# Seven-product (Strassen) gate and up projections in a hybrid decoder block, with all final rows after the last product

## The chip, the cores and the metric

The kernel runs on one core of one Trainium2 chip. The metric is the device time of one execution in microseconds (us), from runs repeated on the same chip; the kernel before takes 1517.94 us (median of 3 runs, 1517.23 to 1519.09). In the profile the engines are PE (TensorE, matmuls), PEld (its weight loads), DVE (VectorE), ACT (ScalarE), POOL (GpSimd) and SP (SyncE, which issues the DMAs).

## The reference

A decoder block on 1024 tokens of width 1024, all in float32. The change touches only its second part, the SwiGLU feed-forward layer with 2816 features, and the layer norm behind it:

```python
# token mixing (projection, convolution, windowed attention, gates, w_out), then
x = layer_norm(ALPHA * x + mix, ln1_g, ln1_b)
hid = silu(x @ w_gate) * (x @ w_up)        # (1024, 2816)
ffn = hid @ w_down                         # (1024, 1024)
x = layer_norm(ALPHA * x + ffn, ln2_g, ln2_b)
```

## The kernel before

Every product of two float32 matrices is made of three matmuls in a reduced-mantissa format: each operand is split into a high part (ACT copies it to that format) and a low part (the difference, made by POOL for weights and by DVE for activations), and high x high, high x low and low x high are added up in PSUM (`product`, lines 971 to 979). Activations lie channels by tokens, as `act_hi` and `act_lo`: 8 tiles of 128 channels, 1024 tokens in two halves of 512.

The feed-forward part works in 11 groups of two feature blocks of 128. For one group the gate and the up weights of both blocks are four tiles of 128 features (`gate_up`, L1132; `s` = 0 to 3, even for gate). A unit is one of these against one half of the tokens: 8 channel tiles x 3 = 24 matmuls of 128x512, so a group has 8 units or 192 matmuls. Behind each pair of units ACT takes the tanh (`silu`, L621), DVE makes gate times up (`hidden`, L896), ACT its high part and DVE its low part. `down` (L1141) then multiplies the two hidden blocks into the output: 16 units (8 output tiles x 2 halves) of 2 x 3 = 6 matmuls, 96 in all, and after each one DVE adds the bank to the residual `res` (`add_down`, L920). Each weight tile is loaded by SP (`load_ffn`), copied by ACT (`ffn_high_part`, L572) and subtracted by POOL (`ffn_low_part`, L400), one group ahead. All engines run their own instruction streams in order and wait for each other through semaphores.

The order on TensorE is: output projection of the mixing part (L1128), first-half units of group 0, into which the statistics of the first layer norm are woven (`mean`, `variance`, `spread`, L1094 to L1115), second-half units of group 0, `down` of group 0, first-half units of group 1, and so on. Before that norm's second half DVE runs `scale_residual(0)` (L866, L894), eight operations that bring the first half of the residual to its scaled and biased form; `scale_residual(1)` (L917) stands between `hidden(0, 0, 1)` and `hidden(0, 1, 0)`, and unit 15's addition to the residual (L881) behind `scale_residual(0)`.

The last group is different. Its output is made as finished rows (tokens on partitions), `last_rows` (L1173): per row block of 128 tokens and half of the channels four transposes of the residual and six matmuls of the last two hidden blocks. `row_stats`, `row_centre` and `row_scale` (DVE, ACT, DVE) and one POOL addition turn them into the output, which SP stores. The list `LAST` (L83) weaves rows 0, 1 and 2 between the four last second-half units; rows 3 to 7 come after them.

Of the kernel before, what the change touches and what calls it, by code (L numbers as in the profile page):

```python
# [21 lines left out]
F32R = mybir.dt.float32r  # L22
# [4 lines left out]
P = 128  # L27
# [32 lines left out]
def head_schedule():  # L60
# [4 lines left out]
    for u in range(2 * NT):  # L65
# [17 lines left out]
LAST = [("unit", 0), ("rows", 0), ("unit", 1), ("silu", 0), ("rows", 1), ("unit", 2), ("rows", 2), ("unit", 3),  # L83
        ("silu", 1)] + [("rows", i) for i in range(3, NB)]
# [13 lines left out]
def build(nc, x, w_in, conv_w, sinks, w_out, ln1_g, ln1_b, w_gate, w_up, w_down, ln2_g, ln2_b, out):  # L98
    ctx = ExitStack()
    with ctx:  # L100
# [27 lines left out]
        sb(ctx, "line_up", [P, 120])  # L128
# [41 lines left out]
        ln2_rows = sb(late, "ln2_rows", [P, 2, D])  # L170
        sb(late, "spare", [P, HALF])
        raw_b = sb(late, "raw_b", [P, 2, DT, P])
# [6 lines left out]
        with ExitStack() as st:  # L179
# [4 lines left out]
            raw_d = sb(st, "raw_d", [P, 2, D])  # L184
            hid_hi = sb(st, "hid_hi", [P, 2, S], F32R)
            hid_lo = sb(st, "hid_lo", [P, 2, S], F32R)
            tanh_g = sb(st, "tanh_g", [P, 2, HALF])
            hid = sb(st, "hid", [P, 2, HALF])
# [27 lines left out]
        n_hi_s, n_lo_s, scaled_s = sem("norm_hi_done"), sem("norm_lo_done"), sem("residual_scaled")  # L216
        fw_in = [sem(f"ffn_w_landed{i}") for i in range(6)]
# [38 lines left out]
        def ffn_raw(s):  # L256
            return raw_b[:, s] if s < 2 else raw[:, s - 2] if s < 4 else raw_d[:, s - 4]
# [6 lines left out]


# [19 lines left out]
        ROW_BANKS = [4, 6, 4, 6, 0, 2, 4, 6]  # L285

        def row_out(i):

            return raw_b[:, i % 4].rearrange("p t c -> p (t c)") if i % 4 < 2 else raw_d[:, i % 4 - 2]

        def row_banks(i):
            return ps[:, ROW_BANKS[i]:ROW_BANKS[i] + 2, :]


        @block.sync
        def _(sp):
# [21 lines left out]
            def load_ffn(g, s):  # L318
                if s < 4:
                    w = (w_gate, w_up)[s % 2]  # L320
                    src = w[0, :, bass.ds(g * (2 * P) + P * (s // 2), P)].rearrange("(t p) c -> p t c", p=P)
                else:
                    src = w_down[0, bass.ds(g * (2 * P) + P * (s - 4), P), :]
                sp.dma_start(ffn_raw(s), src).then_inc(fw_in[s], 16)

            for v in range(OUT_TILES):
                sp.wait_ge(w_lo_s, IN_TILES + v - 1)
                load_w(v % 2, w_out, P * (v % DT))
                if v == DT:
                    sp.wait_ge(merge_s, 2 * NKV)  # L330
                    load_ffn(0, 0)
                    load_ffn(0, 1)
            for s in (2, 3):
                sp.wait_ge(w_lo_s, IN_TILES + OUT_TILES - 3 + s)
                load_ffn(0, s)
            sp.wait_ge(out_s, OUT_TILES)
            load_ffn(0, 4)
# [881 lines left out]
```

## Time and profile before

| | |
|---|---|
| time, median of 3 | 1517.94 us |
| the profiled execution's own time | 1517.19 us |
| its span, first to last instruction | 1515.3 us |
| TensorE busy | 1491.6 us, 98% of the span, 6898 matmuls |
| VectorE, ScalarE, GpSimd busy | 46%, 28%, 26% |
| granted TensorE clock, mean | 0.994 |
| DMA, mean | 53 GB/s |

A matmul's length in the trace (0.39 us) holds its way through the array; the next one starts before it ends. What a matmul costs in a dense stream is the distance from start to start. A length with "x2" behind it is that of two merged instructions. The number in brackets at a row's end is the time for which the engine sat idle before, and who released it.

### The profile page before, as it was taken

Reading aid. Unit: us, or ns where it says so; the run is one execution under the profiler, and the core shown is the slowest. Engines: PE = TensorE matmul, PEld = TensorE weight load, DVE = VectorE, ACT = ScalarE, POOL = GpSimd, SP = SyncE. Lnnn points to the kernel's source line nnn. Section 1 sums busy time; section 2 is a strip of 40 time slices with the busy share of each in tenths; the row PEclk is TensorE's granted clock in tenths of the full one; section 3 lists DMA queues with packets and bytes.
Section 4 is the critical chain, followed back from the end, with each engine's and each line's share of the span. In section 5 each row is a group of like instructions: output and inputs, shape, how many; then the busy total and the mean of one; then the engine's idle time right before and its main releaser. Section 6 shows DMA issues by size and latency. Waiting matters only on the chain.

```text
span 1515.3 us, 18733 instructions
## 1 busy us (share of the span) xinstructions
PE 1491.6 (98%) x6898; PEld 1241.3 (82%) x6898; DVE 696.5 (46%) x1063; ACT 429.7 (28%) x803; POOL 396.5 (26%) x187
## 2 busy tenths in 40 slices
PE   9999999999999999989989999999999999999997
PEld 7888888888888888868868888888888888888885
DVE  3227662766366636679677231323323132332335
ACT  3424332433243324342444111211112121111223
POOL 2121132113211321136743121303213031221303
PEclk9999999999999999999999999999999999999999
DMA  5111111111111111113331110202111020211002
GB/s 168 56 50 34 42 42 47 36 42 42 45 38 42 42 44 39 42 42 111 97 98 55 57 55 28 83 0 83 49 34 55 28 83 12 71 55 55 0 14 98
DMA packets 127754, 80.07 MB, mean 53 GB/s; under 512 B 7792, under 2 KB 122480, under 8 KB 127728
## 3 DMA queue, kind: packets, MB, share of 16 engines
q1 hardware_dynamic: 127728, 79.73, 17.5%
q8 instruction: 16, 0.26, 0.1%
q14 instruction: 10, 0.08, 0.0%
HBM read 75.53 MB, written 4.19 MB: 53 GB/s over the span
## 4 chain that ended last, share of the span: by engine, by line
PE 96%; DVE 3%; ACT 1%; issue 0%; POOL 0%; ACTq 0%; DVEq 0%; POOLq 0%
PE ps L976 29%; PE ps L978 29%; PE ps L977 29%; PE ps L1085 2%; PE ps L1076 2%; PE ps L1068 1%; PE ps L1067 1%; DVE act_lo L850 1%; DVE m_lo L819 0%; DVE res L869 0%; DVE bn L939 0%; PE ps L991 0%; DVE res L860 0%; DVE raw_d L953 0%; PE ps L999 0%
## 5 line engine op out<-in xcount | busy, mean ns | idle before, releaser
L976 PE MATMUL ps<-act_hi,w_hi 128*128 128x512 f32 x1184 | 463.1, 391 | 1.1 <-DVE act_lo L674 1.1
L978 PE MATMUL ps<-act_hi,w_lo 128*128 128x512 f32 x1184 | 461.1, 389 | 0.0
L977 PE MATMUL ps<-act_lo,w_hi 128*128 128x512 f32 x1184 | 461.0, 389 | 0.0
L382 POOL TENSOR_TENSOR w_lo<-raw,w_hi 128x1024 fp32r<-128x1024 f32 x54 | 131.9, 2443 | 506.7 <-ACT w_hi L469 506.7
L978 PEld LDWEIGHTS ps<-act_hi,w_lo 128*128 128x128 f32 x1184 | 222.3, 188 | 46.7
L976 PEld LDWEIGHTS ps<-act_hi,w_hi 128*128 128x128 f32 x1184 | 222.4, 188 | 45.9 <-issue 1.3
L977 PEld LDWEIGHTS ps<-act_lo,w_hi 128*128 128x128 f32 x1184 | 222.5, 188 | 44.5
L923 DVE TENSOR_TENSOR res<-res,ps 128x512 f32<-128x512 f32 x160 | 109.5, 687 | 94.2 <-PE ps L978 94.2
L402 POOL TENSOR_TENSOR w_lo_b<-raw_b,w_hi_b 128x1024 fp32r<-128x1024 f32 x22 | 52.5, 2407 | 372.9 <-ACT w_hi_b L575 372.9
L976 PE MATMUL ps<-act_hi,w_hi_b 128*128 128x512 f32 x352 | 138.2, 393 | 0.0
L977 PE MATMUL ps<-act_lo,w_hi_b 128*128 128x512 f32 x352 | 137.3, 390 | 0.0
L978 PE MATMUL ps<-act_hi,w_lo_b 128*128 128x512 f32 x352 | 137.2, 390 | 0.0
L976 PE MATMUL ps<-hid_hi,wd_hi 128*128 128x512 f32 x320 | 124.5, 389 | 0.0
L977 PE MATMUL ps<-hid_lo,wd_hi 128*128 128x512 f32 x320 | 124.5, 389 | 0.0
L978 PE MATMUL ps<-hid_hi,wd_lo 128*128 128x512 f32 x320 | 124.5, 389 | 0.0
L901 DVE SCALAR_TENSOR_TENSOR hid<-tanh_g,ps 128x512 f32<-128x512 f32 x44 | 30.3, 688 | 169.3 <-ACT tanh_g L625 169.0
L905 DVE TENSOR_TENSOR hid<-hid,ps 128x512 f32<-128x512 f32 x44 | 30.3, 688 | 160.6 <-PE ps L978 160.3
L627 ACT ACTIVATE hid_hi<-hid 128x512 fp32r<-128x512 f32 x44 | 27.8, 632 | 232.0 <-DVE hid L905 232.0
L402 POOL TENSOR_TENSOR wd_lo<-raw_d,wd_hi 128x1024 fp32r<-128x1024 f32 x22 | 52.4, 2405 | 131.9 <-ACT wd_hi L575 131.9
L977 PEld LDWEIGHTS ps<-act_lo,w_hi_b 128*128 128x128 f32 x352 | 66.4, 189 | 14.3 <-issue 0.5
L976 PEld LDWEIGHTS ps<-act_hi,w_hi_b 128*128 128x128 f32 x352 | 66.4, 189 | 14.3 <-issue 0.5
L978 PEld LDWEIGHTS ps<-act_hi,w_lo_b 128*128 128x128 f32 x352 | 66.3, 188 | 13.8
(144 smaller groups left out, 1915.4 us busy)
## 6 DMA issues: line engine op xcount, KB each, us to landing
raw<-in_w_in SPq DMA_DIRECT2D x52, 512.0 KB, 3.8
raw_d<-in_w_down SPq DMA_DIRECT2D x22, 512.0 KB, 3.3
raw<-in_w_out SPq DMA_DIRECT2D x16, 512.0 KB, 3.6
raw_b<-in_w_gate SPq DMA_DIRECT2D x11, 512.0 KB, 3.8
raw_b<-in_w_up SPq DMA_DIRECT2D x11, 512.0 KB, 3.9
raw<-in_w_gate SPq DMA_DIRECT2D x11, 512.0 KB, 3.9
raw<-in_w_up SPq DMA_DIRECT2D x11, 512.0 KB, 4.0
xs<-in_x SPq DMA_DIRECT2D x8, 512.0 KB, 8.2
```

What stands on the lines that cost most here:

```text
L382: pool.tensor_tensor(w_lo[:, slot], raw[:, slot], fp(w_hi[:, slot]), ALU.subtract).then_inc(w_lo_s, 1)
L402: pool.tensor_tensor(ffn_lo(s), ffn_raw(s), fp(ffn_hi(s)), ALU.subtract).then_inc(fw_lo_s, 1)
L627: act.activation(hid_hi[:, t, half(h)], hid[:, t], ACT.Copy, scale=0.5).then_inc(silu_s, 1)
L850: dve.scalar_tensor_tensor(out=act_lo[:, m, half(q)], in0=res[:, m, half(q)], scalar=lnb[:, m:m + 1], in1=fp(act_hi[:, m, half(q)]), op0=A ...
L901: dve.scalar_tensor_tensor(out=hid[:, t], in0=tanh_g[:, t], scalar=1.0, in1=ps[:, 2 * t, :], op0=ALU.add, op1=ALU.mult).then_inc(hid_s, 1)
L905: dve.tensor_tensor(hid[:, t], hid[:, t], ps[:, 2 * t + 1, :], ALU.mult).then_inc(hid_s, 1)
L923: dve.tensor_tensor(res[:, m, half(h)], res[:, m, half(h)], ps[:, 4 + v % 4, :], ALU.add).then_inc(add_s, 1)
L976: pe.matmul(bank, w_h(t), a_hi(t), start=(t == 0), stop=False)
L977: pe.matmul(bank, w_h(t), a_lo(t), start=False, stop=False)
L978: last = pe.matmul(bank, w_l(t), a_hi(t), start=False, stop=(t == tiles - 1))
L1076: last = pe.transpose(ps[:, TURN + kb, blk(g)], prob[:, g, blk(kb)], ident[:])
L1085: last = pe.matmul(ps[:, OUT, :], vs[:, n - 1 + kb, :], part[:, kb], start=(kb == kbs[0] and part is pt_hi), stop=(kb == 1 and part is pt_lo))
```

## The change

Of the 11 groups, group 0 stays as it was. The 20 feature blocks of groups 1 to 10 ("pairs": the gate and the up tile of one block) are computed by one level of the seven-product scheme (Strassen's, in Winograd's form). The 2 x 2 blocks of the left matrix are gate and up weights by first and second half of the channels (A11, A12, A21, A22, each 512 channels by 128 features), those of the right one the two halves of the channels by the two halves of the tokens. Seven products of 4 channel tiles x 3 = 12 matmuls stand for eight, so 84 matmuls in place of 96 for a feature block. Around them:

- Sums of right blocks are made once, after group 0's norm: on DVE `token_sums` (five operations on 128x512 for each of 4 tiles) and `depth_difference` (4, from the third on each waits for the POOL subtraction two before), on ACT 16 copies to the high format, on POOL 8 subtractions. One right block replaces `act_hi`/`act_lo` of the first four channel tiles, second token half.
- Sums of left blocks are made for every feature block on POOL (4 operations on 128x512); ACT makes 7 high parts of 128x512 and POOL 7 low parts, into a ring of four, in place of two of 128x1024 each.
- The products land in four PSUM banks (BX, BY, BZ, BW); ACT copies the first one out, DVE combines them with 7 operations, then `tanh`, gate times up and the split go on as before (5 more on DVE, 4 on ACT). TensorE waits in front of products 0, 1, 3, 4 and 6 for a bank to be read.
- The down projection stays the same, after every second feature block. Its weights now come through one buffer `raw_d` in place of two.
- `scale_residual` is gone; the scale is folded into the first `add_down`, the bias into the last.
- All eight `last_rows` follow the last product.

```diff
-LAST = [("unit", 0), ("rows", 0), ("unit", 1), ("silu", 0), ("rows", 1), ("unit", 2), ("rows", 2), ("unit", 3),
-        ("silu", 1)] + [("rows", i) for i in range(3, NB)]
+PAIRS = 2 * (NG - 1)
+FIRST_HIGH, SECOND_SUM, SECOND_LOW, THIRD_DIFF, FIRST_LOW, FIRST_SUM, FOURTH_DIFF = range(7)
+U2, U3, UP0, GATE0, HID0, LOW0, UP1, PART1, SUM1, GATE1, HID1, LOW1 = range(1, 13)
...
@@ SP @@
-            sp.wait_ge(out_s, OUT_TILES)
-            load_ffn(0, 4)
-            load_ffn(0, 5)
+            sp.wait_ge(stat_s, 5)
+            load_down(0)
+            sp.wait_ge(wd_lo_s, 1)
+            load_down(1)
+            sp.wait_ge(last_lo_s, 4)
+            for c in (A11, A21, A22, A12):
+                load_block(c, 2)
...
@@ POOL, per feature block @@
+                pool.tensor_tensor(w_sum[:, 0], wide(block_raw(A21)), wide(block_raw(A22)), ALU.add).then_inc(sum_s, 1)
+                pool.tensor_tensor(w_sum[:, 1], w_sum[:, 0], wide(block_raw(A11)), ALU.subtract).then_inc(sum_s, 1)
+                low(FIRST_HIGH)
+                low(SECOND_SUM)
+                low(SECOND_LOW)
+                pool.tensor_tensor(wide(block_raw(A21)), wide(block_raw(A11)), wide(block_raw(A21)),
+                                   ALU.subtract).then_inc(sum_s, 1)
+                low(THIRD_DIFF)
+                low(FIRST_LOW)
+                pool.tensor_tensor(w_sum[:, 1], wide(block_raw(A12)), w_sum[:, 1], ALU.subtract).then_inc(sum_s, 1)
+                low(FIRST_SUM)
+                low(FOURTH_DIFF)
...
@@ POOL, once, before the pairs @@
+            down_low_part(0, 0, 0)
+            for t in range(4):
+                pool.wait_ge(dhi_s, t + 1)
+                pool.tensor_tensor(a3_lo[:, t], w_sum[:, t % 2], fp(a3_hi[:, t]), ALU.subtract).then_inc(dlo_s, 1)
+            down_low_part(0, 0, 1)
...
@@ ACT, once @@
+            for t in range(4):
+                act.wait_ge(asum_s, 3 * t + 1)
+                act.activation(a1_hi[:, t], u3[:], ACT.Copy).then_inc(ahi_s, 1)
+                act.wait_ge(asum_s, 3 * t + 2)
+                act.activation(a2_hi[:, t], w_sum[:, 0], ACT.Copy).then_inc(ahi_s, 1)
+            act.wait_ge(out_s, OUT_TILES)
+            down_high_part(0, 0, 0)
+            silu(1, 0)
+            for t in range(4):
+                act.wait_ge(diff_s, t + 1)
+                act.activation(a3_hi[:, t], w_sum[:, t % 2], ACT.Copy).then_inc(dhi_s, 1)
+            down_high_part(0, 0, 1)
+            act.wait_ge(f_s, 8)
...
...
@@ ACT, per feature block, even ones (odd ones: the next block's parts come last) @@
+                first_copy(i, c)
+                product_high(i, c, 4)
+                down_high_part(i, 2 * (c // 2) + 2, c % 2)
+                product_high(i, c, 5)
+                product_high(i, c, 6)
+                    product_high(i, c + 1, 0)
+                    gate_tanh(i, c, 0)
+                    product_high(i, c + 1, 1)
+                    hidden_high(i, c, 0)
+                    product_high(i, c + 1, 2)
+                    product_high(i, c + 1, 3)
+                    gate_tanh(i, c, 1)
+                    hidden_high(i, c, 1)
...
@@ DVE, once @@
             hidden(0, 1)
+            for t in range(4):
+                token_sums(t)
+            hidden(1, 0)
+            for t in range(4):
+                depth_difference(t)
+            hidden(1, 1)
...
@@ PE @@
+            def down(i, c, h, m):
                 if m == 0:
+                    pe.wait_ge(wd_lo_s, i * 4 + (2 * c + 2))
...
+            def pair_product(i, c, j):
+                if j == FIRST_HIGH:
+                    pe.wait_ge(pair_s, before + GATE0)
+                elif j == SECOND_SUM:
+                    pe.wait_ge(pair_s, before + SUM1)
+                elif j == THIRD_DIFF:
+                    pe.wait_ge(pair_s, now + U2)
+                elif j == FIRST_LOW:
+                    pe.wait_ge(s1_s, i * 4 + (c + 1))
+                elif j == FOURTH_DIFF:
+                    pe.wait_ge(pair_s, now + U3)
...
-            for step, n in LAST:
-                if step == "unit":
-                    second_half(NG - 1, n)
-                elif step == "rows":
-                    last_rows(n)
+            for n in range(NB):
+                last_rows(n)
```


## Rows read from the trace of the kernel before

**Rows 1.** The page: busy shares, granted clock in 40 slices, shares of the last chain.
```profile
PE 1491.6 (98%) x6898; PEld 1241.3 (82%) x6898; DVE 696.5 (46%) x1063; ACT 429.7 (28%) x803; POOL 396.5 (26%) x187
...
PEclk9999999999999999999999999999999999999999
...
PE 96%; DVE 3%; ACT 1%; issue 0%; POOL 0%; ACTq 0%; DVEq 0%; POOLq 0%
```

**Rows 2.** The timeline at a unit's end: start, length, engine, line, operation, idle before.
```profile
1007.58 0.39 PE L978 MATMUL ps<-act_hi,w_lo_b 128*128 128x512 f32 x1
...
1007.81 0.39 PE L976 MATMUL ps<-act_hi,w_hi 128*128 128x512 f32 x1
...
1008.10 0.69 DVE L905 TENSOR_TENSOR hid<-hid,ps 128x512 f32<-128x512 f32 x1 [4.03 <-PE ps L978]
...
1008.82 0.63 ACT L627 ACTIVATE hid_hi<-hid 128x512 fp32r<-128x512 f32 x1 [5.57 <-DVE hid L905]
```

**Rows 3.** All instructions of line 923 on VectorE: lengths in ns, first and last start.
```profile
L923 DVE TENSOR_TENSOR res<-res,ps x160: 679/687/689, 825.1 to 1432.3; 128x512 f32<-128x512 f32 x160
```

**Rows 4.** Groups by line, 1000 to 1400 us: count, busy us, mean ns, idle before.
```profile
L402 POOL TENSOR_TENSOR wd_lo<-raw_d,wd_hi 128x1024 fp32r<-128x1024 f32 x12 | 28.5, 2397 | 65.6 <-ACT wd_hi L575 65.6
...
L625 ACT ACTIVATE tanh_g<-ps 128x512 f32<-128x512 f32 x25 | 15.0, 598 | 97.5 <-PE ps L978 97.5
...
L575 ACT ACTIVATE w_hi<-raw 128x1024 fp32r<-128x1024 f32 x12 | 11.9, 1043 | 0.0
```

**Rows 5.** The timeline of GpSimd, 742 to 780 us.
```profile
754.37 1.28 POOL L415 TENSOR_TENSOR acc<-acc,res 128x512 f32<-128x512 f32 x1
755.62 2.85 POOL L426 TENSOR_TENSOR wd_lo<-raw,wd_hi 128x1024 fp32r<-128x1024 f32 x1
...
770.92 1.46 POOL L415 TENSOR_TENSOR acc<-acc,res 128x512 f32<-128x512 f32 x1
775.71 1.26 POOL L415 TENSOR_TENSOR acc<-acc,res 128x512 f32<-128x512 f32 x1 [3.33 <-DVE res L881]
```

**Rows 6.** The timeline of VectorE, 740 to 860 us.
```profile
754.39 1.81 DVE L850 SCALAR_TENSOR_TENSOR act_lo<-res,lnb,act_hi 128x512 fp32r<-128x512 f32 x1
756.13 0.73 DVE L860 SCALAR_TENSOR_TENSOR res<-res,lng,ps 128x512 f32<-128x512 f32 x1
756.79 2.23 DVE L850 SCALAR_TENSOR_TENSOR act_lo<-res,lnb,act_hi 128x512 fp32r<-128x512 f32 x1
...
768.83 6.20 DVE L869 TENSOR_SCALAR res<-res,lnb 128x512 f32<-128x512 f32 x8
774.96 0.67 DVE L881 SCALAR_TENSOR_TENSOR res<-res,ps 128x512 f32<-128x512 f32 x1
...
808.88 0.69 DVE L907 SCALAR_TENSOR_TENSOR hid_lo<-hid,hid_hi 128x512 fp32r<-128x512 f32 x1 [0.70 <-ACT hid_hi L627]
```

**Rows 7.** The timeline of TensorE, 760 to 800 us.
```profile
777.12 2.05 PE L1097 MATMUL ps<-acc,mean_of 128*128 128x512 f32 x2 [5.18 <-POOL acc L415]
...
779.39 0.63 PE L977 MATMUL ps<-act_lo,w_hi_b 128*128 128x512 f32 x1
```

**Rows 8.** The timeline of TensorE, 799 to 803 us.
```profile
801.09 0.39 PE L976 MATMUL ps<-act_hi,w_hi_b 128*128 128x512 f32 x1
```

**Rows 9.** The timeline of TensorE, 1486.2 to 1491 us.
```profile
1486.63 0.60 PE L1187 MATMUL ps<-ident,res 128*128 128x128 f32 x4
...
1488.46 0.60 PE L1187 MATMUL ps<-ident,res 128*128 128x128 f32 x4
```

**Rows 10.** The timeline of VectorE, 1440 to 1515 us.
```profile
1498.65 1.29 DVE L939 BATCH_NORM_STATS2 bn<-ps 128x6 f32<-128x512 f32 x2
...
1507.00 1.29 DVE L939 BATCH_NORM_STATS2 bn<-ps 128x6 f32<-128x512 f32 x2
```

**Rows 11.** DMA issues: queue, count, KB each, median us from issue to landing.
```profile
raw_d<-in_w_down SPq DMA_DIRECT2D x22, 512.0 KB, 3.3
...
ln_rows<-in_ln_b SPq DMA_DIRECT2D x1, 512.0 KB, 6.0
```

More of the change, by code:

```diff
@@ L168, in build @@
             sq = sb(st, "sq", [P, 2, HALF])
[L170 to L172 removed]
+        u3 = sb(late, "u3", [P, HALF])
+        w_sum = sb(late, "w_sum", [P, 2, HALF])
+        raw_d = sb(late, "raw_d", [P, D])
+        with ExitStack() as st:
+            raw_b = sb(st, "raw_b", [P, 2, DT, P])
+        t_g = sb(late, "t_g", [P, 2, HALF])
+        u_st = sb(late, "u_st", [P, 2, HALF])
         with ExitStack() as st:
@@ new lines, in _ @@
+            down_high_part(0, 0, 0)
[6 more added lines that the diff above has]
+            for t in range(4):
+                act.wait_ge(asum_s, 3 * t + 3)
+                act.activation(act_hi[:, t, half(1)], fourth[:, t * HALF:(t + 1) * HALF], ACT.Copy).then_inc(last_hi_s, 1)
@@ L648, in row_centre @@
+            act.wait_ge(f_s, 8)
+            for j in range(4):
+                product_high(0, 0, j)
+            with act.Fori(0, (NG - 2) // 2) as i:
+                for c in range(4):
+                    pair_act(i, c)
+            for c in range(4):
+                pair_act((NG - 2) // 2, c, c < 3)
             def row_centre(i):
@@ L935, in row_stats @@
+            with dve.Fori(0, (NG - 2) // 2) as i:
+                for d in range(2):
+                    pair(i, 2 * d)
+                    pair(i, 2 * d + 1, lambda v: add_down(i, d + 1, v, "plain"))
+            last = (NG - 2) // 2
+            pair(last, 0)
+            pair(last, 1, lambda v: add_down(last, 1, v, "biased"))
+            pair(last, 2)
+            pair(last, 3)
             def row_stats(i):
@@ new lines, in _ @@
+            for s in range(4):
+                pe.wait_ge(hid_s, 3 * (s // 2) + 1 + s % 2)
+                gate_up(1, s, (lambda t: pe.wait_ge(n_lo_s, DT + t + 1)) if s == 0 else None)
+            for h in range(2):
+                for m in range(DT):
+                    down(0, 0, h, m)
+            def pair_product(i, c, j):
+                n = 7 * c + j
+                before = i * 48 + STEPS_OF * c
+                now = i * 48 + STEPS_OF * (c + 1)
+                pe.wait_ge(pl_s, i * 28 + (n + 1))
+                if j == FIRST_HIGH:
[8 more added lines that the diff above has]
+                    pe.wait_ge(pair_s, now + U3)
+                bank = {FIRST_HIGH: BX, SECOND_SUM: BY, SECOND_LOW: BW, THIRD_DIFF: BY, FIRST_LOW: BX, FIRST_SUM: BZ,
+                        FOURTH_DIFF: BY}[j]
+                out, on = ps[:, bank, :], j in (THIRD_DIFF, FIRST_LOW)
+                for t in range(4):
+                    hi, lo = ring(w_hi, n)[:, t], ring(w_lo, n)[:, t]
+                    b_hi, b_lo = right(j, t)
+                    pe.matmul(out, hi, b_hi, start=(t == 0 and not on), stop=False, skip_group_check=True)
+                    pe.matmul(out, hi, b_lo, start=False, stop=False, skip_group_check=True)
+                    last = pe.matmul(out, lo, b_hi, start=False, stop=(t == 3), skip_group_check=True)
+                last.then_inc(prod_s, 1)
```

460 lines of the change are left out of this document (325 added, 135 removed).

## The prediction

> **What bounds the kernel now.** I read the page first: TensorE is busy 98% of the span, its granted clock stands near full in all 40 slices, and the chain that ended last is TensorE for 96% [rows 1]. So the question is how many matmuls there are, what one costs, and where TensorE would have to wait. A busy share says nothing of the cost of one, so I went to the timeline: starts lie 0.23 us apart while each row is 0.39 long [rows 2]. The exact pitch comes from the downward additions: 160 of them, the first at 825.1, the last at 1432.3 [rows 3]. The last lies 15 units of 6 matmuls behind the first of its own group, and nine groups of 288 matmuls lie between the firsts: 9 x 288 + 90 = 2682 matmuls in 607.2 us is 0.2264, and allowing 0.7 us by which the very first addition ran late, 0.2267 us each (12 matmuls: 2.72). That is the pitch of a stream without a hole across nine groups and their loop ends; TensorE truly bounds this stretch.
>
> **Part 1: the matmuls that go.** 12 per feature block, 20 blocks: 240 x 0.2267 = 54.4 us, all on the path. The bounds are narrow, since product and down matmuls have the form of those removed: 54 to 55.
>
> **Part 2: `scale_residual(0)` goes.** Its eight operations take DVE 768.83 to 775.03, then comes unit 15's addition, 0.67 us, then POOL's last channel sum 775.71 to 776.97 [rows 5, 6], and TensorE's `mean` starts at 777.12 after 5.18 us idle [rows 7]. Without them the addition is through at about 769.6. Next late is POOL: its sixth sum starts at 770.92 behind a weight subtraction [rows 5]; two sums of 1.3 and 0.1 between them end at 773.6, and `mean` starts at 773.8: 3.3 us gained. After that idle time the granted clock is at its lower level, 1.2 GHz: a matmul ends 0.43 behind the one before instead of 0.23 [rows 7] for some five of them, and the two of `mean` take 2.05. With under 2 us idle some of this may go: 0 to 1.9 us, I take 1.0. Sum 4.3 (bounds 3.3 to 5.2).
>
> **Part 3: sums of the activations, before the pairs.** This is the dear part. The clock of before less 4.3 from here. Second-half units started at 801.09 [rows 8], now 796.8, and their 96 matmuls end at 818.6. DVE is through with `hidden(0, 1)` at 809.57 - 4.3 = 805.3 [rows 6]. `token_sums`: dependent DVE operations of 0.69 [rows 2] need about 0.8 each with the wait; per tile three of them, then two low parts that find ACT's copies (0.63, starting 0.03 behind their source [rows 2]) done, 3.7 us; four tiles: 14.8, to 820.1. ACT then still has `down_high_part` (1.04 [rows 4]), done at 819.5, and the tanh (0.60 [rows 4]); `hidden(1, 0)` takes until 823.0. Then come the differences: two at once, to 824.3; the third needs POOL's first `a3_lo` (ACT's copy at 824.3, POOL 1.26 [rows 5]) and finds POOL on the second, 826.8; the fourth at 828.2; ACT's last copy 828.8, POOL's last 830.6. Only behind that stands `down_low_part(0, 0, 1)`: ACT's copy at 829.9 (the one buffer was free at 822, and a load lands in 3.3 [rows 11]), POOL's 2.40 [rows 4], from 830.6 to 833.0. The first `down` waits for exactly this. TensorE stands still from 818.6 to 833.1: 14.5 us. Before, a group's `down` found its weights done long ago. I bound it by 10 (dependent operations at 0.66 and no contention) and 20 (a landing of 6.0 [rows 11] and every DVE operation held up by POOL once). The clock afterwards starts low again, as in Part 2: 1.5 us more (0 to 2). The rest of this preparation is hidden: POOL's last subtractions end near 838.6, the pair's four blocks are loaded and summed by 854, and `down` runs until 833.1 + 1.5 + 21.8 = 856.4. The down additions start late, near 836.5, as DVE first ends `hidden(1, 1)`; the fifth down unit, at 838.5, needs one of them: just there.
>
> **Part 4: do the pairs run without holes?** Time 0 is the start of an even block's product 0; product j ends at 2.72(j + 1), and others see it 0.29 later (1008.10 against 1007.81 [rows 2]). POOL's work per block is 11 operations of 1.25 [rows 5] and one of 2.40, 16.2 us against TensorE's 19.0: the fullest engine beside it. Worse, POOL and DVE exclude each other when DVE has two inputs in SBUF. DVE's L850 at 754.39 took 1.81 instead of 0.7: it ran when POOL's operation of 754.37 ended at 755.65; and that of 756.79 took 2.23, until POOL's 2.85 long one (2.40 elsewhere) let go. L860, whose second input is in PSUM, took 0.73 in the middle of it [rows 5, 6]. Five of the twelve DVE operations (HID0, LOW0, GATE1, HID1, LOW1) are of the first kind.
>
> The Trainium skill ("SBUF — State Buffer", Who interferes with whom) says the same as a rule: two SBUF inputs on DVE and a reading GpSimd operation take turns, for a whole instruction. Without such turns the chain below would have about 1.3 us more to spare and the sum would not change.
>
> The tight place is where an odd block follows an even one with no `down` between. POOL: the sixth low part after ACT's copy at 9.1, `down_low_part` until 12.7, first sum 13.95, second 15.35, then DVE's HID0 takes its turn to 16.0, low 0 until 17.2 (TensorE wants it at 19.05), DVE's LOW0 to 17.8, low 1 until 19.05 (wanted at 21.8), low 2 until 20.3, third sum 21.55. ACT: copy 3 22.2, only then the tanh 22.8. DVE: GATE1 after POOL's low 3, 24.1; HID1 24.9; ACT 25.6; LOW1 26.3; U2 of the odd block 27.0. TensorE's product 3 of that block wants U2 at 19.05 + 8.16 = 27.2. So it just fits, with 0.2 us; a further turn lost to POOL costs up to 1.25 once in each of the ten double blocks: 0 to 12 us, I take 1.0 in all. All other waits have over 1.4 us: first copy 26.2 for 29.9, low 4 28.1 for 29.9, LOW0 of the odd block 37.6 at worst for `down` at 38.1, LOW1 43.5 for its second half at 49; the additions follow from 43.5 and stay ahead of the four banks. While `down` runs (21.8 us) the next block's first four parts are made. What covers Part 1 is thus this slack; where it's gone, products wait one by one.
>
> **Part 5: the end.** Before: row 3 starts on TensorE at 1486.63, the span ends 28.7 later; the three woven rows cost 2 x 1.83 = 3.66 each on TensorE [rows 9]: 39.7 us. After the last product, now: SUM1, tanh, GATE1, HID1, copy, LOW1, 4.55 us; DVE's first `row_stats` starts there (TensorE's row 0 is done at 3.7). Rows then follow each other at the pace of the DVE and ACT chain, (1507.00 - 1498.65) / 2 = 4.18 [rows 10], seven times 29.3, and from the last one's start to the end of the span are 8.3: 42.2. Loss 2.5 us (1 to 5): three rows more at 4.18 instead of 3.66, and the start. The rows of the norm's parameters land in 6.0 [rows 11], within the last seven-product block.
>
> **Sum.** -54.4 - 4.3 + 14.5 + 1.5 + 1.0 + 2.5 = -39.2: span 1515.3 to 1476.1. The profiled execution took 1517.19, 1.9 more than its span, so 1478.0; the median of the runs is 0.75 above that execution: 1478.7, so 1479 us.
>
> **The rivals.**
> A, main: TensorE stays the bound in the pairs, one stall of some 14 us before them. 1479, from 1470 to 1488. Chance 0.66.
> B: the turns of POOL and DVE, or a product's low part, come late in each double block. For it speaks the 0.2 us of slack, and that TensorE's stall moves everything behind it; against it that U2 late by a turn only costs that turn. 1 to 3 us for each of ten, where A has 0.1: 1488 to 1508, likeliest 1494. Chance 0.17.
> C: no real stall at the preparation (DVE or the down weights sooner than worked out): 1479 less 10 to 15, 1464 to 1469. For it only that each step of Part 3 is an estimate; against, the order of the streams. Chance 0.09.
> D, slower: every DVE operation and POOL exclude each other, those with an input in PSUM too. Then the 38.1 us of a double block hold some 24.8 us of POOL work and 24 x 0.66 = 15.8 of DVE: 40.6, and the ring's slack is used up by handoffs, 5 us or more per double block; from 4 us each on the 39 are gone. 1529. Against it stands the 0.73 us of L860 [rows 6]. Chance 0.04.
> E: the change doesn't do what it says: TensorE's pitch in the products rises above 0.227, as with accumulation into a bank that is read between, by 0.01 x 1680 = 17 us: 1496. The same form of matmul in `down` switches banks every 6 without loss. Chance 0.04.
>
> The Trainium skill ("TensorE: Matmul & The Clock Gate", Why this matters for your kernels) warns that idle gaps between bursts of matmuls bring the slow clock; by that rule the stall of Part 3 is followed by a slow start, and the trace agrees at 777 us.
>
> **Range and chances.** A with its bounds, B's likelier half and the upper end of C make 1467 to 1500: this leaves out the end of C, the upper third of B, D. A measurement of this kernel can tell about 0.2% (3 us). Faster 0.95, same 0.01, slower 0.04.
>
> **What would show it.** Part 1: 6658 matmuls instead of 6898 at an unchanged pitch of 0.227. Part 2: `mean` starts about 3 us sooner after the last unit. Part 3: TensorE idle 14 us ahead of the first `down`, released by POOL's `wd_lo`. Part 4: a double block with its `down` takes 168 + 96 = 264 matmuls, 59.9 us, from one to the next; more means B, and the idle row names its releaser. Part 5: rows 4.2 us apart, the last product 42 us before the end. The prediction is wrong if a double block takes over 61 us, or if the first `down` starts within 5 us of the last unit.

## The result and the profile after

The changed kernel takes 1477.92 us (median of 4 runs, 1475.69 to 1479.79) against 1518.4 us (4 runs) beside it: a ratio of 0.9735, 95% interval 0.9723 to 0.9746. The forecast was 1479 us. The profiled execution is the slowest of the four, 1479.79 us with a span of 1478.0; a second profile of the same kernel, called after_again below, has a span of 1474.3.

The page of after (busy time and share of each engine, then the chain that ended last); TensorE has 240 matmuls fewer than in [rows 1] and still is busy for 97% of the span:

```profile
PE 1440.5 (97%) x6658; PEld 1198.4 (81%) x6658; DVE 798.7 (54%) x1194; ACT 486.7 (33%) x935; POOL 602.4 (41%) x375
...
PE 90%; DVE 4%; POOL 2%; ACT 2%; issue 1%; DMA 0%; SPq 0%; ACTq 0%; DVEq 0%; POOLq 0%
```

Some stretches of after: first the end of the norm, the stall and the first down projection, then two of the 60 us stretches of the pairs, the first and the last but one. Columns: length, busy time of TensorE, its weight loads, VectorE, ScalarE and GpSimd with the number of instructions in brackets, then granted clock, DMA share and GB/s:

```profile
775.00:800.00 25.00, 24.26 (x110) 19.80 (x109) 17.29 (x26) 12.74 (x19) 5.76 (x4) 0.93 0.07 22
...
821.00:835.00 14.00, 0.50 (x3) 0.21 (x2) 7.38 (x11) 7.51 (x13) 10.06 (x7) 0.60 0.11 37
835.00:860.00 25.00, 25.00 (x99) 20.41 (x100) 12.70 (x19) 3.05 (x5) 14.01 (x11) 0.88 0.32 95
860.00:920.00 60.00, 60.00 (x266) 49.70 (x265) 28.87 (x41) 15.95 (x26) 33.85 (x24) 1.00 0.18 53
...
1340.00:1400.00 60.00, 60.00 (x266) 49.70 (x265) 29.96 (x40) 15.86 (x26) 33.75 (x24) 1.00 0.18 53
```

From 860 to the end of the last product TensorE has no hole in any stretch. The ScalarE copy that each feature block has once gives the distance of the blocks (durations in ns, then the first and the last start):

```profile
L820 ACT ACTIVATE u_st<-ps x20: 579/592/598, 862.5 to 1423.3; 128x512 f32<-128x512 f32 x20
```

20 copies, the first at 862.5, the last at 1423.3. The 560.8 us between them serve below to compare kernels; they are no exact pitch, since the first copy starts 3.0 behind the start of its block on TensorE (859.49) and the last 6.2 (1417.09). The pitch is in TensorE's own rows: 2544 matmuls from the start of the first product at 859.49 to the end of the last at 1436.13, 0.2267 each: to four digits the pitch that the prediction takes from [rows 3]. The holes that there are, by TensorE's waits (releaser, us in total, times, longest):

```profile
PE ps L1289 <- POOL wd_lo L543: 13.5, 1, 13.5
PE ps L1289 <- DVE m_lo L1042: 5.4, 3, 2.0
PE ps L1410 <- POOL acc L504: 1.8, 1, 1.8
...
PE ps L1418 <- DVE sq_acc L1056: 0.7, 1, 0.7
```

The 13.5 us are the stall ahead of the first down projection; the 5.4 us behind `m_lo` are in both kernels. The stall's surroundings on TensorE (start, length, idle before), to be read beside [rows 7, 8]:

```profile
820.91 0.39 PE L1291 MATMUL ps<-act_hi,w_lo 128*128 128x512 f32 x1
834.79 0.79 PE L1289 MATMUL ps<-hid_hi,wd_hi 128*128 128x512 f32 x1 [13.50 <-POOL wd_lo L543]
835.39 0.63 PE L1290 MATMUL ps<-hid_lo,wd_hi 128*128 128x512 f32 x1
...
840.87 0.39 PE L1291 MATMUL ps<-hid_hi,wd_lo 128*128 128x512 f32 x1
```

and the chain that released it, on GpSimd, where the last weight subtraction stands behind four of the activations' (to be read with [rows 5] for its lengths):

```profile
821.46 2.51 POOL L543 TENSOR_TENSOR wd_lo<-raw_d,wd_hi 128x1024 fp32r<-128x1024 f32 x1 [37.45 <-ACT wd_hi L781]
826.17 2.49 POOL L583 TENSOR_TENSOR a_lo<-w_sum,a_hi 128x512 fp32r<-128x512 f32 x2 [2.20 <-ACT a_hi L793]
829.94 2.49 POOL L583 TENSOR_TENSOR a_lo<-w_sum,a_hi 128x512 fp32r<-128x512 f32 x2 [1.29 <-ACT a_hi L793]
832.40 2.34 POOL L543 TENSOR_TENSOR wd_lo<-raw_d,wd_hi 128x1024 fp32r<-128x1024 f32 x1
```

The end, VectorE's `row_stats` of the first rows, answers to [rows 10]:

```profile
1440.44 1.29 DVE L1255 BATCH_NORM_STATS2 bn<-ps 128x6 f32<-128x512 f32 x2
...
1444.63 1.29 DVE L1255 BATCH_NORM_STATS2 bn<-ps 128x6 f32<-128x512 f32 x2
```

The pace is 4.19 us a row, and the last product ends at 1436.13, 41.9 us before the end of the span.

### The profile page after: what moved, and what is told of

Its sections match the earlier page's. It is cut to its first block, busy times and chain, and to the rows that moved or that the text cites. A ratio compares the mean times of both kernels' runs of the same rounds, so it can differ in the third digit from the quotient of the medians.

```text
span 1478.0 us, 19122 instructions
## 1 busy us (share of the span) xinstructions
PE 1440.5 (97%) x6658; PEld 1198.4 (81%) x6658; DVE 798.7 (54%) x1194; ACT 486.7 (33%) x935; POOL 602.4 (41%) x375
## 3 DMA queue, kind: packets, MB, share of 16 engines
HBM read 75.53 MB, written 4.19 MB: 54 GB/s over the span
## 4 chain that ended last, share of the span: by engine, by line
PE 90%; DVE 4%; POOL 2%; ACT 2%; issue 1%; DMA 0%; SPq 0%; ACTq 0%; DVEq 0%; POOLq 0%
PE ps L1289 19%; PE ps L1290 19%; PE ps L1291 19%; PE ps L1505 9%; PE ps L1504 9%; PE ps L1506 9%; PE ps L1398 2%; PE ps L1389 2%; PE ps L1381 1%; PE ps L1380 1%; DVE rows L1269 1%; POOL acc L504 1%; DVE bn L1255 1%; ACT rows L882 1%; DVE m_lo L1042 1%
## 5 line engine op out<-in xcount | busy, mean ns | idle before, releaser
L559 POOL TENSOR_TENSOR w_lo<-raw,w_hi 128x512 fp32r<-128x512 f32 x80 | 108.5, 1357 | 234.8 <-ACT w_hi L814 234.8
L1291 PEld LDWEIGHTS ps<-act_hi,w_lo 128*128 128x128 f32 x864 | 162.5, 188 | 34.4
L1289 PEld LDWEIGHTS ps<-act_hi,w_hi 128*128 128x128 f32 x864 | 162.8, 188 | 33.6 <-issue 1.3
L1290 PEld LDWEIGHTS ps<-act_lo,w_hi 128*128 128x128 f32 x864 | 162.7, 188 | 32.1
L1289 PE MATMUL ps<-hid_hi,wd_hi 128*128 128x512 f32 x320 | 125.9, 393 | 13.5 <-POOL wd_lo L543 13.5
L1504 PE MATMUL ps<-a_hi,w_hi 128*128 128x512 f32 x240 | 93.4, 389 | 0.0
L1505 PE MATMUL ps<-a_lo,w_hi 128*128 128x512 f32 x240 | 93.4, 389 | 0.0
L1506 PE MATMUL ps<-a_hi,w_lo 128*128 128x512 f32 x240 | 93.4, 389 | 0.0
L559 POOL TENSOR_TENSOR w_lo<-w_sum,w_hi 128x512 fp32r<-128x512 f32 x60 | 81.8, 1371 | 11.3 <-ACT w_hi L814 11.3
L1289 PEld LDWEIGHTS ps<-hid_hi,wd_hi 128*128 128x128 f32 x320 | 60.7, 190 | 26.6 <-POOL wd_lo L543 13.9
L612 ACT ACTIVATE w_hi<-raw 128x1024 fp32r<-128x1024 f32 x54 | 57.0, 1056 | 70.4 <-PE ps L1291 69.8
```

The lines of the kernel that those rows point to most:

```text
L559: pool.tensor_tensor(wide(ring(w_lo, n)), src, fp(wide(ring(w_hi, n))), ALU.subtract).then_inc(pl_s, 1)
L612: act.activation(w_hi[:, slot], raw[:, slot], ACT.Copy).then_inc(w_hi_s, 1)
L1289: pe.matmul(bank, w_h(t), a_hi(t), start=(t == 0), stop=False)
L1290: pe.matmul(bank, w_h(t), a_lo(t), start=False, stop=False)
L1291: last = pe.matmul(bank, w_l(t), a_hi(t), start=False, stop=(t == tiles - 1))
L1504: pe.matmul(out, hi, b_hi, start=(t == 0 and not on), stop=False, skip_group_check=True)
```

## The experiments

All ratios are against the kernel before, with 95% intervals; "against the changed kernel" compares medians (1476.91 us for after_again in the first group of runs). Differences of 1 us are at the edge of what the runs tell.

**The base.** after_again is the changed kernel unaltered, no diff.

> The changed kernel once more, as the base of the three beside it on the same chip. Theory: 1478 us within 3, with some 13.5 us of idle TensorE ahead of the first down product.

Measured: 1476.91 us (5 runs, 1476.09 to 1478.65), ratio 0.9733 (0.9720 to 0.9746), TensorE idle 13.5 us behind `wd_lo` as before. Its span is 3.7 us shorter than that of the first profile: `token_sums` begins at 805.4 instead of 807.8, and the first product at 855.8 instead of 859.5. The clock makes all of that. Behind the last of the three waits for `m_lo`, ahead of everything that the change touches, the first profile has twelve matmuls at a distance of 0.43 us, this one eight and the profile of before seven; behind the wait of 0.7 us for `variance` the first profile has six and this one none; behind the stall it is thirteen and about seven. The three places make 0.7, 1.7 and 1.3 us. The first of them in the first profile:

```profile
678.39 0.80 PE L1289 MATMUL ps<-m_hi,w_hi 128*128 128x512 f32 x1 [1.80 <-DVE m_lo L1042]
...
683.68 0.45 PE L1289 MATMUL ps<-m_hi,w_hi 128*128 128x512 f32 x1
```

**1. The weights first.** Is the stall only that of the two down weight tiles?

```diff
@@ ScalarE @@
+            act.wait_ge(out_s, OUT_TILES)
+            down_high_part(0, 0, 0)
             for t in range(4):
+                if t == 3:
+                    down_high_part(0, 0, 1)
                 act.wait_ge(asum_s, 3 * t + 1)
...
-            act.wait_ge(out_s, OUT_TILES)
-            down_high_part(0, 0, 0)
             silu(1, 0)
...
-            down_high_part(0, 0, 1)
@@ GpSimd @@
             down_low_part(0, 0, 0)
+            down_low_part(0, 0, 1)
...
-            down_low_part(0, 0, 1)
```

> Changed kernel, in which the two down weight tiles of group 0 are copied (ScalarE) and subtracted (GpSimd) before and between the sums of the activations, not after them. Nothing else moves. Theory: TensorE starts down at about 821, right behind the last unit, does four of its units and then waits for VectorE's first addition, which still comes after hidden(1, 1) near 837: the stall changes its name and shrinks from 13.5 to about 11 us, and 5 to 6 us are gained in all, since four units of down (5.4 us) lie before it. Rival: the weights are all that is late; then the whole stall and its slow clock go, 16.5 us.

Measured: 1477.38 us (4 runs), ratio 0.9733 (0.9718 to 0.9748): nothing gained against the changed kernel, where I had expected 5 to 6 us. The stall did change its name; TensorE, the four early down units and the wait for VectorE's first addition:

```profile
820.29 0.50 PE L1290 MATMUL ps<-hid_hi,wd_hi 128*128 128x512 f32 x1 [1.26 <-POOL wd_lo L543]
...
838.91 0.80 PE L1290 MATMUL ps<-hid_hi,wd_hi 128*128 128x512 f32 x1 [12.88 <-DVE res L1181]
```

But the idle time did not shrink (1.3 + 12.9 us). The weights' subtraction on GpSimd now lies beside `token_sums`. VectorE and GpSimd, same kernel:

```profile
806.24 2.77 DVE L1133 SCALAR_TENSOR_TENSOR w_sum<-res,lnb,u 128x512 f32<-128x512 f32 x1
...
818.05 2.74 DVE L1131 TENSOR_TENSOR u<-res 128x512 f32<-128x512 f32 x1
```

```profile
805.90 2.56 POOL L543 TENSOR_TENSOR wd_lo<-raw_d,wd_hi 128x1024 fp32r<-128x1024 f32 x1 [22.53 <-ACT wd_hi L781]
817.72 2.52 POOL L543 TENSOR_TENSOR wd_lo<-raw_d,wd_hi 128x1024 fp32r<-128x1024 f32 x1 [9.25 <-ACT wd_hi L781]
```

An operation with two inputs in SBUF that takes 0.75 elsewhere took 2.77, ending 0.5 behind GpSimd's 2.56 long one, and another that takes 0.69 took 2.74. That puts 4 us into the chain that ends in the first addition; later waits take up some of it, and the addition comes 32.7 us behind the start of `token_sums` (838.18 - 805.52) instead of 30.0.

The expected 5 to 6 us were also never there. Counted from the start of `token_sums`, the changed kernel's down projection starts at 27.0 us (834.79 - 807.77). With the weights early its fifth unit waits for the end of the first addition, at 30.7: four units of work (5.4 us) are done by then, but the rest starts 3.7 us later, so that only 1.7 us were to be gained. The turns took 2.7, and the first product comes 51.4 us behind the start of `token_sums` (856.9 - 805.5) in place of 50.4 in after_again. Neither theory holds in its size: the weights are not all that is late, and with VectorE's order as it is, moving them alone has little to give.

**2. Weights first and VectorE's work in another order.** The edit of experiment 1, and on VectorE the following; ScalarE and GpSimd follow, with `silu(1, 1)` and its copies ahead of those of `a3`:

```diff
             hidden(1, 0)
-            for t in range(4):
-                depth_difference(t)
-            hidden(1, 1)
...
-            for v in range(2 * DT):
-                add_down(0, 0, v, "first")
+            for v in range(4):
+                add_down(0, 0, v, "first")
+            hidden(1, 1)
+            for v in range(4, 2 * DT):
+                add_down(0, 0, v, "first")
+                if v < DT:
+                    depth_difference(v - 4)
```

> As weights_early, and VectorE takes four down additions before hidden(1, 1) and puts the four depth differences between the next additions; ScalarE and GpSimd follow that order. Theory: no stall of over 1 us is left ahead of the pairs, 13.7 us of idle time and 2.9 us of slow clock are gained: 16.6 us less than the changed kernel, 1461. Rival: the work is only pushed to the start of the pairs, where products wait for it: gain under 10 us.

Measured: 1468.78 us (4 runs), ratio 0.9672 (0.9657 to 0.9687), 8.1 us less than the changed kernel; half of what was expected. From the start of `token_sums` to the first product it takes 40.3 us (808.4 to 848.7), against 50.4 in after_again and 51.7 in the first profile; without any hole it would be 35.1. TensorE's waits name what is left:

```profile
PE ps L1294 <- DVE res L1176: 2.0, 2, 1.0
...
PE ps L1294 <- POOL wd_lo L543: 1.3, 1, 1.3
...
PE ps L1509 <- DVE inv L1194: 0.8, 1, 0.8
```

Four short waits in place of a long one, 4.1 us, at a granted clock of 1.00, and in this kernel too two VectorE operations of 2.77 and 2.74 us took turns with GpSimd. So the stall is that of a packed VectorE: between the start of `token_sums` and the first product it is busy for 35.6 of the 40.3 us here (32.6 of 51.7 in the first profile), where TensorE's own work takes 35.1, and each turn with GpSimd lengthens it. As the profiles differ in the clock before this place, the 10 to 11 us of the stretch and the 8.1 us of the medians are not the same number. It was not pushed into the pairs (560.4 us between first and last copy, as before).

**3. What the stall's slow clock costs.** 56 matmuls into a bank that is free fill most of the idle stretch:

```diff
+            for n in range(56):
+                pe.matmul(ps[:, 4, :], act_hi[:, 0, 0:P], act_hi[:, 0, half(0)], start=True, stop=True)
             for h in range(2):
                 for m in range(DT):
                     down(0, 0, h, m)
```

> Changed kernel with 56 extra matmuls of 128x512 into a bank that nobody reads, between group 0's last unit and its first down product: 12.7 us of work inside the stall of 13.7. Theory: TensorE keeps the granted clock of 2.4 GHz, the first down products run at 0.227 from the start and 2.9 us are gained although 56 matmuls are added. Rival: the slow start of down has another cause (the first reading of new weights): no gain, or a loss where the extra matmuls outlast the stall.

Measured: 1475.37 us (5 runs, 1475.25 to 1475.59), ratio 0.9720 (0.9707 to 0.9733). 1.5 us less than after_again, with 56 matmuls more. The windows (columns as above) of after_again and then of this kernel:

```profile
832.00:842.00 10.00, 9.58 (x36) 7.82 (x37) 6.02 (x9) 1.27 (x2) 5.80 (x5) 0.82 0.28 78
```

```profile
818.00:832.00 14.00, 14.00 (x64) 11.51 (x62) 7.88 (x11) 8.30 (x14) 8.75 (x6) 1.00 0.11 37
832.00:842.00 10.00, 9.01 (x40) 7.23 (x39) 6.48 (x10) 1.33 (x3) 6.70 (x5) 1.00 0.20 58
```

TensorE now waits 1.0 us for `wd_lo`, the granted clock stays at 1.00 over the whole stretch and the slow start is gone, so its cause is the idle time. I had expected 2.9 us, the figure of the first profile; 1.5 us is what the medians give, and all five runs lie below all five of after_again. This is also the kernel whose runs lie closest together (0.3 us, where the changed kernel's spread over 4). How much of that is chance in five runs is not shown: the slow matmuls behind `m_lo` and `variance` come before the filled stretch, so the filling can't have changed them.

**4. How near GpSimd is to being the bound in the pairs.** One more operation in odd, then in even feature blocks (`c % 2 == 0` in the second kernel):

```diff
+                if c % 2 == 1:
+                    pool.tensor_tensor(w_sum[:, 0], wide(block_raw(A21)), wide(block_raw(A22)), ALU.add).then_inc(twice_s, 1)
+                    pool.wait_ge(twice_s, i * 2 + (c // 2 + 1))
                 pool.tensor_tensor(w_sum[:, 0], wide(block_raw(A21)), wide(block_raw(A22)), ALU.add).then_inc(sum_s, 1)
```

> Changed kernel in which GpSimd does the first weight sum of every odd feature block twice, one operation of 128x512 (1.25 us, 1.4 with the wait) more in the tight place of the prediction. Theory: U2 of the odd block was ready 0.5 us before TensorE wanted it, so product 3 now starts some 0.9 us late in each of ten double blocks: 9 us more than the changed kernel, 1487. Rival: GpSimd works ahead by a ring of four and one operation is hidden: within 1 us of the changed kernel.

> The same extra operation in every even block instead, whose first sums fall into the down products (21.8 us). Theory: hidden, within 1 us of the changed kernel. Rival: GpSimd's total load is what counts: as much slower as with the odd blocks.

Measured: odd 1486.14 us (4 runs), ratio 0.9793 (0.9778 to 0.9808); even 1477.93 us (4 runs), ratio 0.9736 (0.9721 to 0.9751). 9.2 us more than the changed kernel for the odd blocks, 1.0 for the even ones, and first to last copy takes 570.3 us instead of 560.8: 0.95 us per double block. The size and the rule (the second of two neighbouring blocks is tight, the one behind a down projection is free) are as worked out. The place is another. (SUM1, HID0, LOW0 and U2 are steps of VectorE's work on a feature block, by the names in the diff of the change.) VectorE and TensorE of the kernel with the odd ones:

```profile
1424.79 0.69 DVE L1229 TENSOR_TENSOR u_st<-u_st,ps 128x512 f32<-128x512 f32 x1
1424.86 0.39 PE L1510 MATMUL ps<-act_hi,w_lo 128*128 128x512 f32 x1
...
1425.62 0.47 PE L1508 MATMUL ps<-a_hi,w_hi 128*128 128x512 f32 x1 [0.38 <-DVE u_st L1229]
```

```profile
PE ps L1508 <- DVE u_st L1229: 2.1, 10, 0.4
```

L1229 is SUM1 of the even block, for which product 1 of the odd one waits: the late low part of LOW0 (1.83 us in this profile, in turns with GpSimd) holds up VectorE's next three operations. Product 1 starts 0.76 behind its predecessor instead of 0.23; product 3, for which I had seen the tight place, is another 0.17 late (1430.92 to 1431.32). In the changed kernel itself it is the other way round. There SUM1 ends 1.8 us before product 1 starts, and U2 ends 0.5 us before product 3 does, so that U2 is the tighter one:

```profile
1417.28 0.69 DVE L1225 TENSOR_TENSOR u_st<-u_st,ps 128x512 f32<-128x512 f32 x1 [0.31 <-PE ps L1506]
...
1419.81 0.39 PE L1504 MATMUL ps<-a_hi,w_hi 128*128 128x512 f32 x1
...
1424.05 0.68 DVE L1209 TENSOR_TENSOR u_st<-u_st,ps 128x512 f32<-128x512 f32 x1
...
1425.24 0.39 PE L1504 MATMUL ps<-a_hi,w_hi 128*128 128x512 f32 x1
```

The extra operation of 1.4 us delays SUM1 by more than itself, by 2.2 us against TensorE's products: LOW0 starts 1.6 later and takes 1.83 beside GpSimd in place of 1.01.

**5. The order of the rows at the end.**

```diff
+            row_stats(0)
             for n in range(NB):
-                row_stats(n)
+                if n + 1 < NB:
+                    row_stats(n + 1)
                 row_scale(n)
```

> Changed kernel in which VectorE takes the statistics of row n+1 before it scales row n. Theory: the end is paced by the chain VectorE, ScalarE, VectorE at 4.18 us a row; with it broken the pace is TensorE's 3.66 (or 3.7, as the scale and GpSimd's addition of 2.40 take turns), 7 x 0.5 = 3.4 us less. Rival: TensorE or the stores pace the rows already: no change.

Measured: 1473.69 us (5 runs), ratio 0.9712 (0.9698 to 0.9725), 3.2 us less than after_again (whose runs belong to another group; the ratios differ by 0.0021, which is 3.2 us too). The pace of the rows, to be read from the starts of L1269 against 4.18 before:

```profile
1441.02 1.28 DVE L1269 SCALAR_TENSOR_TENSOR rows<-rows,inv,raw 128x1024 f32<-128x1024 f32 x1
...
1444.67 1.28 DVE L1269 SCALAR_TENSOR_TENSOR rows<-rows,inv,raw 128x1024 f32<-128x1024 f32 x1
...
1448.32 1.28 DVE L1269 SCALAR_TENSOR_TENSOR rows<-rows,inv,raw 128x1024 f32<-128x1024 f32 x1
...
1464.33 3.52 DVE L1269 SCALAR_TENSOR_TENSOR rows<-rows,inv,raw 128x512 f32<-128x512 f32 x2
```

3.65 us, TensorE's own time for a row [rows 9]: the mechanism is as expected, but the 3.2 us are not all its work. In the profiles the time from the end of the last product to the end of the span falls from 41.9 to 39.9 us (1432.3 to 1472.2), by 1.9 only. Between the first and the last start of L1269 5.5 us are gained (28.8 to 23.3). The first one comes 1.45 us later behind the last product (8.75 against 7.30), as two rows' statistics go before it, and the last takes 3.52 for two halves, in turns with GpSimd's addition, where it was 1.41. The other 1.3 us of the medians lie ahead of the last product, where this edit changes nothing; that the sum came out near the expected 3.4 is luck.

**6. Both.** The edits of experiments 2 and 5 together.

> reordered and rows_ahead in one kernel. Theory: the two gains lie at different places of the path and add up: 16.6 + 3.4 = 20 us below the changed kernel, 1458. Rival: less than the sum.

Measured: 1465.31 us (5 runs, 1464.73 to 1466.83), ratio 0.9655 (0.9642 to 0.9668). 11.6 us below the changed kernel; 8.1 and 3.2 had been the parts. They add up within what the runs can tell, and what is missing from the 1458 expected is what experiment 2 had fallen short by. Of all kernels here this is the fastest.

**7. The first half's residual.** The prediction priced the missing eight operations at 4.3 us. First only moved, in the kernel before:

```diff
-                if v == DT + 6:
-                    scale_residual(0)
...
+            scale_residual(0)
             dve.wait_ge(res_s, OB + OUT_TILES)
             centre(1)
```

> The kernel before, with only the eight operations of the first residual scaling moved from before unit 15's addition to behind it. Theory: they fall into the time in which VectorE waits for the mean; mean starts 3.3 us sooner, and 2.5 to 4 us are gained. Rival: centre, which follows them on VectorE, is what is late next, and nothing is gained.

Measured: 1519.34 us (11 runs) against 1518.15, ratio 1.0009 (1.0000 to 1.0018): nothing gained, perhaps 1 us lost. The rival holds. TensorE and VectorE:

```profile
774.91 1.10 PE L1096 MATMUL ps<-acc,mean_of 128*128 128x512 f32 x2 [2.02 <-POOL acc L415]
...
776.36 0.63 PE L977 MATMUL ps<-act_hi,w_lo_b 128*128 128x512 f32 x1
...
787.83 1.92 PE L1104 MATMUL ps<-mean_of,sq_acc 128*128 128x1 f32 x16 [2.04 <-DVE sq_acc L833]
```

```profile
770.40 8.74 DVE L869 TENSOR_SCALAR res<-res,lnb 128x512 f32<-128x512 f32 x8
779.06 3.67 DVE L838 TENSOR_TENSOR res<-res,ps 128x512 f32<-128x512 f32 x6
```

`mean` did start sooner, 774.91 with 2.0 us of idle time, but the eight operations took 8.74 us (6.20 in [rows 6]; GpSimd worked beside them in both kernels, for longer here) and ended just when centring had begun before. `variance`, which had not waited before, then waited 2.0 us for VectorE, and TensorE ran slowly for some time behind both waits. Then left out altogether, which leaves the first half of the residual unscaled and without its bias:

```diff
-                if v == DT + 6:
-                    scale_residual(0)
...
-            dve.wait_ge(scaled_s, 2 * DT)
+            dve.wait_ge(scaled_s, DT)
```

> The kernel before without the eight operations of scale_residual(0) (the first half of the residual is then neither scaled nor biased: the output is another). This is the part of the change that the prediction priced at 4.3 us (3.3 of a sooner mean, 1.0 of clock). Moving them behind unit 15's addition had put them in front of centre, which then started no sooner. Theory: with them gone, mean starts 3.3 us sooner and centre follows it; of the clock's part nothing is safe, as the idle time that is left still lets it fall in some executions: 2 to 3.5 us faster than the kernel before. Rival: variance, which then waits for VectorE's squares, takes it back: under 1 us.

Measured: 1513.03 us (8 runs) against 1517.43, ratio 0.9974 (0.9963 to 0.9984): 4.0 us less by the ratio (4.4 by the medians), 2.4 to 5.6 by its interval.

**8. The rows' order alone.**

```diff
-LAST = [("unit", 0), ("rows", 0), ("unit", 1), ("silu", 0), ("rows", 1), ("unit", 2), ("rows", 2), ("unit", 3),
-        ("silu", 1)] + [("rows", i) for i in range(3, NB)]
+LAST = [("unit", 0), ("unit", 1), ("silu", 0), ("unit", 2), ("unit", 3), ("silu", 1)] + [("rows", i) for i in range(NB)]
```

> The kernel before, with rows 0, 1 and 2 not woven between the last four units but after them, as in the changed kernel. Theory: 2.2 to 2.5 us slower, three rows more at the pace of 4.18 instead of 3.66 and the later start. Rival: weaving gains nothing or costs something (table loads on ScalarE between tanh and square root): same or faster.

Measured: 1518.71 us (11 runs) against 1518.15, ratio 1.0004 (0.9995 to 1.0013): not to be told from no change. The profile shows more than the times: the last unit ends at 1476.62 and the span is 1517.4, so the end takes 40.8 us against 39.7 before. VectorE starts the first row here 2.2 us behind the last unit, but then waits for TensorE with the row's second half:

```profile
1478.20 0.69 DVE L906 SCALAR_TENSOR_TENSOR hid_lo<-hid,hid_hi 128x512 fp32r<-128x512 f32 x1 [0.70 <-ACT hid_hi L626]
1478.81 0.69 DVE L938 BATCH_NORM_STATS2 bn<-ps 128x6 f32<-128x512 f32 x1
1480.48 0.70 DVE L938 BATCH_NORM_STATS2 bn<-ps 128x6 f32<-128x512 f32 x1 [0.97 <-PE ps L1191]
```

In the changed kernel it starts 4.3 us behind (1440.44 - 1436.13), because SUM1 and the tanh behind it come first, and doesn't wait: its statistics of row 0 end 1.0 us later behind the last product than here. So of the 2.2 us that the end really costs in the changed kernel, half is the order of the rows and half the longer chain behind the last product. In the expectation of this run I had put all of it on the order.

## Why the prediction was right

1479 us was said and 1477.92 measured. The profiled execution was 1479.79, the median is 1.9 below it, and the forecast had put the median 0.75 above: that the number comes out within 1.1 us is partly luck, as what an execution loses to the slow clock makes 3.7 us between the two profiles of this kernel. Term by term, in us of the span, the first profile beside the forecast:

| term | forecast | measured | from |
|---|---|---|---|
| 240 matmuls | -54.4 | -54.4 | pitch 0.2267 in both |
| slow clock behind the last wait for `m_lo` | no term | +0.9 | twelve slow matmuls against seven in before; the last unit before `mean` is 0.9 later |
| first residual scaling gone | -4.3 | -2.6 | second-half units start at 799.37 - 0.9 against 801.09 |
| idle ahead of the first down | +14.5 | +13.6 | 821.14 to 834.79 |
| slow clock behind it | +1.5 | +2.9 | 24.7 us for 96 matmuls of 21.8 |
| holes in the pairs | +1.0 | 0 | 2544 matmuls without one |
| the end | +2.5 | +2.2 | 41.9 against 39.7 |
| sum | -39.2 | -37.4 | 1515.3 to 1478.0 |

The second row is no effect of the change: both kernels start the same matmul behind the last wait for `m_lo` at 678.4, and only the number of slow ones behind it differs. The -2.6 of the third row holds 1.7 us of slow matmuls behind `variance`. In after_again, whose span is 3.7 us shorter, three terms differ: +0.2 there, -4.3 for the residual, since the units end at 818.7, and +1.6 for the slow clock (23.4 us). Experiments 7 and 3, over all their runs, give -4.0 and +1.5 for the last two. So the forecast of each is right in size, and the first profile is one of the longer executions.

**Part 1** is exact, and it is the part that carries the result: the pitch doesn't depend on the new order of banks, on products that add to a bank that is read between, or on a loop body of twice the length. That rules out rival E.

**Part 2** was right in its size (4.3 against 4.0 when measured alone) and in its first step: `mean` starts at 774.69 - 0.9 = 773.8, as worked out. Its split was not: in the kernel without the eight operations `mean` starts 3.3 us sooner and the clock gives back 1.7 where 1.0 was taken, but `variance` now waits 0.7, which had no term. Nor is it a gain that any way of clearing the place would give, as the first half of experiment 7 expected: it hangs on the operations being gone, since centring stands behind them on the same engine. And of the waits that are left there, 1.8 us for `mean` and 0.7 us for `variance`, the second was followed by slow matmuls in one profile and by none in the other.

**Part 3** found a stall, its place (`wd_lo` of group 0, on GpSimd, behind the four `a3_lo`) and its length from the order of three streams. The measured chain follows it step by step: `token_sums` takes 14.0 where 14.8 was said, and from its start to the end of the last low part it is 27.0 (807.77 to 834.74) where 27.7 was (805.3 to 833.0). What it missed is what would be late next if the weights were not. The prediction named the wait for the additions "just there" but never asked how the stall would shrink; experiments 1 and 2 answer it: not at all by moving the weights alone, and by 8.1 us of the median by changing VectorE's own order with them.

The rule of the Trainium skill ("SBUF — State Buffer", Who interferes with whom) on turns for a whole instruction holds in every row that I looked at: the operations of 2.77 and 2.74 us in experiment 1 end 0.5 us behind GpSimd's. The same section counts `tensor_scalar`, with one input, among those that can take part; the trace of before agrees, though no run isolates it: the first of the eight `tensor_scalar` operations, at 768.83, took 2.41 us, until just behind the end of GpSimd's operation of 768.56, which took 2.40, where the shortest of them takes 0.47.

**Part 4** came out on the good side of its 0.2 us: in the trace U2 is ready 0.5 us before product 3 starts. Experiment 4 shows that the slack is small: an operation of 1.4 us more costs 0.95 in each double block. That also speaks on rival B, which was near: one GpSimd operation of 512 elements separates it from the main case. The wait that the extra operation opens is SUM1 for product 1, which I had counted among those with room; it has 1.8 us in the changed kernel, but a delay on GpSimd reaches it enlarged by a turn. Rival D is out, as UP1 and PART1 keep their length (0.68 us, all twenty of each) beside GpSimd.

**Part 5** had the size, and its two reasons (more rows at the slower pace, the later start) are both at work; experiment 8 puts about half of the 2.2 us on each.

The rule that idle gaps bring the slow clock ("TensorE: Matmul & The Clock Gate" in the Trainium skill, Why this matters for your kernels) is borne out by experiment 3: with the gap filled the clock stays at 1.00. That the price differs from one execution to the next (seven slow matmuls or thirteen behind the same 13.5 us) I had not reckoned with.

What stays open: why matmuls are slow behind the wait of 0.7 us in one execution and not in the next; and how much of the 5.2 us (40.3 - 35.1) that experiment 2 still loses is due to the turns alone, as no kernel was made that keeps GpSimd silent during `token_sums`.

## What to carry to other kernels

Where TensorE is busy without a hole, fewer matmuls are worth exactly their number times the pitch, as long as every helper engine stays ahead; so price the helpers in the narrowest window between two reads of the same bank, not by their share of the span. The cost of such a change sits in its preparation and its end, and both can be worked out by laying the streams of three engines beside each other from rows of the old trace. Before moving work out of a stall, look at which engine is full there: work put beside a chain that has to take turns with it comes back as waiting, and operations that are moved in front of the next thing that their own engine must do gain nothing. And add up what the move can give, from the moment at which the waiting engine would start again, before building it: in experiment 1 that sum, 1.7 us, would have said beforehand that there was little to win.

## What the runs showed of the hardware

- The price of an idle stretch of TensorE is not fixed. Behind the same 13.5 us the distance of 0.43 instead of 0.23 lasted for 7 matmuls in one execution and 13 in another; behind 0.7 us it came in one, for six, and not in the other. Behind one and the same wait of 1.8 us for `m_lo` it was seven, twelve, eight and fourteen matmuls (before, the first profile of the changed kernel, after_again, experiment 2). The changed kernel's runs spread over 4 us; with the stall filled they lie within 0.3 us.
- VectorE operations with two SBUF inputs waited for the whole of a GpSimd operation even when that had begun only 0.3 us before: 2.77 and 2.74 us in place of 0.75 and 0.69. One with a single input in SBUF (`tensor_scalar`) took 2.41 in place of 0.47 in the same way.
